# Three edits to a two-block kernel: full meta tile in the heads, final norm on three engines, gate and up as separate products

## The reference

```python
# attention: 8 heads, causal, keys are 16 meta tokens and 1024 others
p = softmax(where(kpos <= qpos, s, -inf));  o = p @ v
# experts: 64 of them, each token goes to 2
hh = silu(xb @ w_gate[e]) * (xb @ w_up[e])     # 1024 -> 256
y  = hh @ w_down[e]                            # 256 -> 1024
# end: the two expert rows of a token are added to h by their gates, then
return rmsnorm(h, final_norm_g)[:, N_META:]
```

## Time and profile before

| | |
|---|---|
| median of 3 runs | 2974.53 us (2974.14 to 2975.85) |
| the profiled execution, its own time | 2974.75 us |
| its span in the profile | 2973.0 us |
| TensorE busy | 2624.7 us, 88% |
| VectorE, ScalarE, GpSimd busy | 1038.2, 543.4 and 189.4 us |
| mean of the DMA engines | 190 GB/s |
| pairs of layer 0, first product to last | 1190.5 to 1699.7 us |
| pairs of layer 1, first product to last | 2408.7 to 2919.6 us |
| final norm | 2930.7 us to the end |

### The profile page before, as it was taken

One profiled execution on the slowest core, in us unless ns is written; L12 is line 12 of the kernel. 1 busy time (PEld: TensorE's weight loads), 2 busy tenths in 40 slices (PEclk: granted clock), 3 DMA queues, 4 the chain that ended last, 5 costly groups with the idle time before them and its releaser, 6 DMA issues. The chain is left out here.

```text
span 2973.0 us, 36737 instructions
## 1 busy us (share of the span) xinstructions
PE 2624.7 (88%) x14822; PEld 1477.7 (50%) x14822; DVE 1038.2 (35%) x2424; ACT 543.4 (18%) x1370; POOL 189.4 (6%) x262
## 2 busy tenths in 40 slices
PE   8999999998999997978877789999999978878882
PEld 3444579746888654333333255665665533333330
DVE  2424556556555344201111053444443431111114
ACT  0212455310000011201111031321221111111112
POOL 1000000000000000111111020000000011111100
PEclk9999999998999998988999889999999979999996
DMA  3101010131112154899999860000103479999995
GB/s 109 36 30 56 1 45 4 48 121 41 43 43 111 52 200 186 336 420 420 419 420 417 327 250 15 16 23 8 65 26 135 150 300 421 420 420 419 415 415 233
DMA packets 107724, 565.87 MB, mean 190 GB/s; under 512 B 21377, under 2 KB 21537, under 8 KB 56081
## 3 DMA queue, kind: packets, MB, share of 16 engines
q1 hardware_dynamic: 81216, 502.14, 42.4%
q0 software_dynamic: 21440, 43.51, 3.9%
q10 hardware_dynamic: 4896, 17.83, 1.5%
HBM read 529.06 MB, written 65.01 MB: 200 GB/s over the span
## 5 line engine op out<-in xcount | busy, mean ns | idle before, releaser
L2162 PE MATMUL ex__h_ps<-all__arena,ex__xT 128*64 128x512 f32 x1696 | 525.3, 674 | 170.8 <-DMA all__arena<-in_w_up 114.5
L2162 PEld LDWEIGHTS ex__h_ps<-all__arena,ex__xT 128*64 128x64 f32 x1696 | 169.9, 154 | 472.9 <-issue 468.3
L290 PE MATMUL fr__acc<-X__xT,fr__w 128*128 128x512 f32 x640 | 283.2, 603 | 7.5 <-DMA X__xT<-in_xT 7.5
L2190 DVE TENSOR_TENSOR ex__hs<-ex__sg,ex__h_ps 128x256 f32<-128x256 f32 x64 | 27.0, 421 | 680.6 <-ACT ex__sg L2187 680.3
L1290 PE MATMUL pb__acc<-b__w,all__arena 128*128 128x512 f32 x544 | 245.4, 606 | 9.3 <-POOL pb__eps L1250 9.3
L290 PEld LDWEIGHTS fr__acc<-X__xT,fr__w 128*128 128x128 f32 x640 | 122.6, 193 | 165.9 <-issue 156.6
L2162 PE MATMUL ex__h_ps<-mo__wx,ex__xT 128*64 128x512 f32 x352 | 178.0, 664 | 0.0
L1290 PEld LDWEIGHTS pb__acc<-b__w,all__arena 128*128 128x128 f32 x544 | 102.9, 194 | 129.2 <-issue 118.8
L2176 PE MATMUL ex__y_ps<-b__w,ex__hT 128*64 128x512 f32 x672 | 153.5, 598 | 1.1 <-ACT ex__hT L2193 1.1
L2187 ACT ACTIVATE ex__sg<-ex__h_ps 128x256 f32<-128x256 f32 x64 | 24.6, 384 | 656.2 <-PE ex__h_ps L2162 656.2
L1521 PE MATMUL cm__acc<-all__arena,cw__w 128*128 128x260 f32 x576 | 136.0, 386 | 2.3 <-PEq L84 2.3
(11 more groups left out here) (430 smaller groups left out, 3685.7 us busy)
## 6 DMA issues: line engine op xcount, KB each, us to landing
all__arena<-in_w_gate SPq DMA_DIRECT2D x106, 1024.0 KB, 21.6
all__arena<-in_w_up SPq DMA_DIRECT2D x106, 1024.0 KB, 25.5
b__w<-in_w_down SPq DMA_DIRECT2D x84, 1024.0 KB, 21.0
all__arena<-in_w_down SPq DMA_DIRECT2D x22, 1024.0 KB, 15.8
mo__wx<-in_w_down SPq DMA_DIRECT2D x22, 1024.0 KB, 25.4
mo__wx<-in_w_gate SPq DMA_DIRECT2D x22, 1024.0 KB, 23.9
mo__wx<-in_w_up SPq DMA_DIRECT2D x22, 1024.0 KB, 29.2
all__arena<-s_ys SPq DMA_DIRECT2D x16, 1024.0 KB, 7.7
```

What stands on the lines that cost most here:

```text
L290: last = mm(acc[:, b, c], wbuf[:, b, k], xT[:, k, 512 * c:512 * c + 512], start=(k == 0), stop=(k == KT - 1))
L2162: last = nc.tensor.matmul(h_ps[half, b].rearrange("p (a b) -> p a b", a=2), xT[:, b, k, half], slots[n][:, :, k], start=(k == 0), stop=(k ...
L2190: return nc.vector.tensor_tensor(hs[:, b], sg[:, b], h_ps[:, b, DE:], ALU.mult)
```

## The change

**Heads:** the meta keys are treated as a tile of 128 rows like the others: the transposed tile holds the 16 meta keys and the first 112 keys behind them, and the rows of `vv` that meet those 112 are zero (a memset once). Each group is then one copy. **Experts:** the product is split into `gate_products` and `up_products`, 16 calls of 256 columns each, with semaphores of their own; the down products of pair p-1 move between the two; SP loads gate of both experts when gate is done and up when up is done. ScalarE and VectorE follow this order. PSUM bank 0 holds gate, bank 1 up. **Final norm:** all eight tiles of `h` are loaded ahead, and four instead of three of the expert rows; ScalarE multiplies the tile with the inverted root, VectorE multiplies 384 columns with the gain (two tiles behind), and GpSimd the other 640; the stores move from GpSimd's queue to SP's.

The diff, cut to its core (the rest renames semaphores, passes them on, and makes the same split in code for overfull experts, which holds no product in the profile):

```diff
-            tiles = [(s, META + P * s, P) for s in range(i + 1)] + [(NB, 0, META)]
+            tiles = [(s, META + P * s) for s in range(i + 1)] + [(NB, 0)]
...
-                        at, r = (0, META) if tile == NB else (META + P * tile, P)
+                        at = 0 if tile == NB else META + P * tile
                         for k in range(CT):
-                            last = mm(t_ps[0:r, g % 2, 2 * VD * a:2 * VD * a + 2 * VD], ckv[:, k, at:at + r],
+                            last = mm(t_ps[:, g % 2, 2 * VD * a:2 * VD * a + 2 * VD], ckv[:, k, at:at + P],
                                       wkv[:, j % 2, k, 2:4].rearrange("p a b -> p (a b)"),
...
-                        for a, (s, at, r) in enumerate(group):
-                            last = nc.tensor.transpose(t_ps[0:r, q % 2, P * a:P * a + P], pr[:, h, u % 2, at:at + r], ident[:])
+                        for a, (s, at) in enumerate(group):
+                            last = nc.tensor.transpose(t_ps[:, q % 2, P * a:P * a + P], pr[:, h, u % 2, at:at + P], ident[:])
...
-                    for a, (s, at, r) in enumerate(tiles):
-                        last = mm(o_ps[:, h, 0:P], vv[0:r, s, h], pT[0:r, h, s], start=(a == 0), stop=(a == len(tiles) - 1))
+                    for a, (s, at) in enumerate(tiles):
+                        last = mm(o_ps[:, h, 0:P], vv[:, s, h], pT[:, h, a], start=(a == 0), stop=(a == len(tiles) - 1))
...
-                        full = [s for s, at, r in group if r == P]
-                        if full:
-                            last = nc.scalar.copy(pT[:, h, full[0]:full[-1] + 1].rearrange("p s q -> p (s q)"),
-                                                  t_ps[:, q % 2, 0:P * len(full)])
-                        if len(full) < len(group):
-                            at = P * len(full)
-                            last = nc.scalar.copy(pT[0:META, h, NB], t_ps[0:META, q % 2, at:at + P])
+                        last = nc.scalar.copy(pT[:, h, 4 * g:4 * g + len(group)].rearrange("p s q -> p (s q)"),
+                                              t_ps[:, q % 2, 0:P * len(group)])
...
+                v(V.memset(vv[:, NB].rearrange("p a b -> p (a b)"), 0.0))
...
+    def gate_in(sp, slot, e, loaded):
+        sp.dma_start(slot[:, 0], wg_d[bass.ds(e, 1)].rearrange("a (p k) f -> (a p) k f", k=KT)).then_inc(loaded, 16)
+
+    def up_in(sp, slot, e, loaded):
+        sp.dma_start(slot[:, 1], wu_d[bass.ds(e, 1)].rearrange("a (p k) f -> (a p) k f", k=KT)).then_inc(loaded, 16)
 
...
-        def gate_up_products(b, slots):
+        def gate_or_up_products(c, b, slots):
             for k in range(KT):
                 for n in range(2):
                     half = slice(CAP * n, CAP * n + CAP)
-                    last = nc.tensor.matmul(h_ps[half, b].rearrange("p (a b) -> p a b", a=2), xT[:, b, k, half],
-                                            slots[n][:, :, k], start=(k == 0), stop=(k == KT - 1))
+                    last = nc.tensor.matmul(h_ps[half, c, DE * b:DE * b + DE], xT[:, b, k, half], slots[n][:, c, k],
+                                            start=(k == 0), stop=(k == KT - 1))
             return last
+
...
-            return nc.scalar.activation(sg[:, b], h_ps[:, b, 0:DE], ACT.Silu)
+            return nc.scalar.activation(sg[:, b], h_ps[:, 0, DE * b:DE * b + DE], ACT.Silu)
...
-            return nc.vector.tensor_tensor(hs[:, b], sg[:, b], h_ps[:, b, DE:], ALU.mult)
+            return nc.vector.tensor_tensor(hs[:, b], sg[:, b], h_ps[:, 1, DE * b:DE * b + DE], ALU.mult)
...
+                    sp.wait_ge(m["g_done"], p - RING + 1)
+                    for n in range(2):
+                        gate_in(sp, gu_slots[r][n], p + n * PAIRS_M, g_loaded[r])
                     sp.wait_ge(m["h_done"], p - RING + 1)
                     for n in range(2):
-                        gate_up(sp, gu_slots[r][n], p + n * PAIRS_M, gu_loaded[r])
+                        up_in(sp, gu_slots[r][n], p + n * PAIRS_M, u_loaded[r])
                     sp.wait_ge(m["y_done"], p - RING + 1)
...
-                    pe.wait_ge(gu_loaded[p % RING], 64 * (p // RING + 1))
-                    gate_up_products(p % 2, gu_slots[p % RING]).then_inc(m["h_done"], 1)
+                    pe.wait_ge(g_loaded[p % RING], 32 * (p // RING + 1))
+                    gate_products(p % 2, gu_slots[p % RING]).then_inc(m["g_done"], 1)
+                    if p >= 1:
+                        last_product(p - 1)
+                    pe.wait_ge(u_loaded[p % RING], 32 * (p // RING + 1))
+                    up_products(p % 2, gu_slots[p % RING]).then_inc(m["h_done"], 1)
                     if p + 1 < PAIRS_M:
                         turn(p + 1)
-                    if p >= 1:
-                        last_product(p - 1)
                     pe.wait_ge(m["h_out"], p + 1)
                     turn_hidden(p % 2).then_inc(m["h_turned"], 1)
...
-                    act.wait_ge(m["h_done"], p + 1)
+                    act.wait_ge(m["g_done"], p + 1)
                     silu(p % 2).then_inc(m["silu_done"], 1)
+                    if p >= 1:
+                        y_half(p - 1)
                     if p + 1 < PAIRS_M:
                         rows_out(p + 1)
-                    if p >= 1:
-                        y_half(p - 1)
                     act.wait_ge(m["h_turned"], p + 1)
...
+                    if p >= 1:
+                        y_half(p - 1)
                     dve.wait_ge(m["silu_done"], p + 1)
+                    dve.wait_ge(m["h_done"], p + 1)
                     hidden(p % 2).then_inc(m["h_out"], 1)
                     if p + 1 < PAIRS_M:
                         rows_out(p + 1)
-                    if p >= 1:
-                        y_half(p - 1)
                     if p == 1:
                         gates(dve, v)
...
-    NBUF = 3
+    TT = SEQ // P
...
-        self.hb = part(0, self.NBUF, DM)
-        self.gb = part(3, DM)
+        self.hb = part(0, self.TT, DM)
+        self.gb = part(8, DM)
...
-        for t in range(self.NBUF):
+        for t in range(self.TT):
             sp.dma_start(self.hb[:, t], self.h_in[P * t:P * t + P]).then_inc(self.h_loaded[t], 16)
...
-        NBUF, NOUT = 3, 4
+        NBUF, NOUT = pre.NBUF, 4
+        CUT = 640
         yb, y_loaded = pre.yb, pre.y_loaded
         hb, gb, g_loaded, h_loaded = pre.hb, pre.gb, pre.g_loaded, pre.h_loaded
-        ho = part(15, NOUT, DM)
+        ho = part(17, NOUT, DM)
         sq = ph.sb("sq", [P, DM], mybir.dt.bfloat16)
         ss, rt, rs = (ph.sb(n, [P, 2]) for n in ("ss", "rt", "rs"))
         eps = ph.sb("eps", [P, 1])
-        eps_done, made, squared, rooted, scaled, v_own = (
-            ph.sem(n) for n in ("eps_done", "made", "squared", "rooted", "scaled", "v_own"))
+        eps_done, made, squared, rooted, inverted, normed, scaled, part_scaled, v_own = (
+            ph.sem(n) for n in ("eps_done", "made", "squared", "rooted", "inverted", "normed", "scaled", "part_scaled", "v_own"))
         stored = [ph.sem(f"o{n}_stored") for n in range(NOUT)]
         with nc.Block() as block:
 
             @block.sync
             def _(sp):
                 for t in range(TT):
-                    b = t % NBUF
-                    if t >= NBUF:
-
-                        sp.wait_ge(made, t - NBUF + 1)
-                        sp.dma_start(hb[:, b], h_in[P * t:P * t + P]).then_inc(h_loaded[b], 16)
-                        pre.rows_in(sp, t)
+                    if t + NBUF < TT:
+
+                        sp.wait_ge(made, t + 1)
+                        pre.rows_in(sp, t + NBUF)
+                    sp.wait_ge(scaled, t + 1)
+                    sp.wait_ge(part_scaled, t + 1)
+                    sp.dma_start(D["out"][P * t:P * t + P], ho[:, t % NOUT]).then_inc(stored[t % NOUT], 16)
+                for b in range(NOUT):
+                    sp.wait_ge(stored[b], 16 * ((TT + NOUT - 1 - b) // NOUT))
 
             @block.gpsimd
             def _(pool):
+                pool.wait_ge(g_loaded, 16)
                 for t in range(TT):
-                    pool.wait_ge(scaled, t + 1)
-                    pool.dma_start(D["out"][P * t:P * t + P], ho[:, t % NOUT]).then_inc(stored[t % NOUT], 16)
-                for b in range(NOUT):
-                    pool.wait_ge(stored[b], 16 * ((TT + NOUT - 1 - b) // NOUT))
+                    pool.wait_ge(normed, t + 1)
+                    nc.gpsimd.tensor_tensor(ho[:, t % NOUT, 0:CUT], ho[:, t % NOUT, 0:CUT], gb[:, 0:CUT],
+                                            ALU.mult).then_inc(part_scaled, 1)
 
             @block.scalar
             def _(act):
                 act.wait_ge(eps_done, 1)
                 nc.scalar.activation(rt[:, 1:2], eps[:], ACT.Sqrt)
-                for t in range(TT):
-                    b = t % 2
-                    act.wait_ge(made, t + 1)
-                    if t >= 2:
-                        act.wait_ge(scaled, t - 1)
```

(47 more changed lines are left out.)

39 lines of the change are left out of this document (24 added, 15 removed).

## The result

The changed kernel takes 2946.9 us, the median of 4 runs (2945.6 to 2948.1), against 2974.3 us (2973.6 to 2975.9) before: ratio 0.9907, 95% interval 0.9891 to 0.9923. The forecast was 2962.1 us in a range of 2954 to 2973. The direction was right, the time lies 7 us under the range, and the gain is 27.5 us where 12.2 were forecast.

What follows compares the result with a forecast made beforehand. Weight transfers were taken to pace the experts' stretches, TensorE nearly always busy in the heads. 2973.0 - 8.0 - 7.1 (experts) - 1.5 (heads) + 4.2 (norm) = 2960.6 us profiled, 2962.1 in runs; range 2954 to 2973.

Steps and rivals of the forecast that it cites:

- Mixing products have equal columns: Heads: mixing products keep their column count, so the change was given no effect on their time.
- 1.5 us net: Heads: fewer copies save 2.8 us, wider transposes cost about 1.3; net gain 1.5 us, between -3 and +8.
- The waits of TensorE for ScalarE: Heads: TensorE's waits for ScalarE were to fall by 2 to 3 us.
- E: Rival, chance 0.10: norm's ScalarE multiply or tail is shorter, or heads give their 8 us: 2952 to 2957 us.
- GpSimd's multiply ... fits under 4.57: Norm: GpSimd's 640 columns take 2.2 us at the end, 3 to 4 inside, within a tile's cycle of 4.57.
- VectorE is stretched too: Norm: VectorE's multiply-adds lengthen beside GpSimd, 0.2 us by 5, +1.0 us in all.
- rival B: Norm, chance 0.12: GpSimd blocks VectorE for its whole instruction, second multiply-adds wait, +12 to +24 us: 2974 to 2986 us.
- Rows 12: Profile rows cited for the norm: a VectorE multiply-add of 1.28 us took 1.54 beside GpSimd, argued against full blocking.
- Experts, start: Experts: first down product and its reload come 4.6 us earlier; 4.0 us gained a layer, 8.0 in all.
- Rival D: Experts, chance 0.11: early start is lost as transfers run out again some pairs later; only the ends gain: 2970 us.
- Experts, end: Experts: last down product 8.7 us after the last up lands, against 11.5 and 13.0; gain 7.1 us.
- Rival C: Experts, chance 0.05: 256-column products don't hide weight loads or issue; over 0.33 us for two, TensorE bounds; +190 us at 0.43.

Runs made afterwards that it cites:

- run 2: Kernel before, with only the mixing products reading all 128 rows of the meta tile, transposes and copies unchanged: 2952.0 us, ratio 0.9918.
- run 4: Kernel before, with the second head's mixing starting at its 16-row tile, so both heads' 16-row products stand side by side: 2961.5 us, ratio 0.9952.
- run 1: Kernel before with the whole heads' part of the change alone: 2951.0 us, ratio 0.9921.
- run 3: Kernel before with the heads' part, but mixing products still reading only 16 rows of the meta tile: 2973.4 us, ratio 0.9997.
- run 10: As run 3, but mixing reads 64 rows of the meta tile: 2973.3 us, ratio 0.9996.
- run 8: Changed kernel, with VectorE's part of the norm's gain copied once into PSUM, GpSimd's multiply unchanged: 2943.4 us, ratio 0.9887.
- Run 11: Kernel before with the experts' part alone, but down products left behind the up products and next transposes: 2968.5 us, ratio 0.9977.
- run 5: Kernel before with the final norm's part of the change alone: 2984.9 us, ratio 1.0030.
- run 6: Kernel before with the experts' part of the change alone: 2959.4 us, ratio 0.9946.
- run 7: Changed kernel, with VectorE multiplying all 1024 columns by the gain and GpSimd doing nothing in the norm: 2938.7 us, ratio 0.9872.
- run 9: Changed kernel, with VectorE alone making the norm's sums and scaling, ScalarE only square and root, GpSimd nothing: 2931.0 us, ratio 0.9857.

## Why the prediction was wrong, and where it was right

**Heads: the step that failed.** "Mixing products have equal columns" put mixing at nothing. The columns are equal, the row counts were not: TensorE went 128, 16, 128 rows twice in a block of queries, and each change cost it 0.18 to 0.19 us (runs 2 and 4, and the single products shown above). 32 blocks with four changes are 128 changes, 23.6 us, the term that is missing. It was to be seen before: the two forms of L1887 differed by 38 ns at equal columns, and two blocks of different length left 0.7 us that the instruction count did not explain. The profile page's own group of that line mixes them ("+1 forms", 290 ns), so they have to be asked for by form. What I did price there fits: 1.5 us net was forecast for copies and transposes, runs 1 and 2 differ by 1.5, and run 3 gives 0.9; but unchanged heads scatter by 0.9, so this is no close test, and the way to it was wrong. The waits of TensorE for ScalarE did not fall by 2 to 3 us as forecast: in the heads those of L1877 and L1887 are 16.5 us in all after the change and were 17.0. The time lies under all the rivals too: the lowest, E, began at 2952 us and gave the heads 8 us.

Not all changes are gone: counted over the order of products in the trace, the heads' stretch had 208 changes between 128 rows and fewer, and has 80 now, at 64-row products. At one of them, among the score products, the start-to-start time again grows from 0.12 to 0.22 us. No run took these away.

The Trainium skill has the rule, and I did not weigh it: the page TensorEngine Tiling (Array Packing) (section "Key Properties") says that changing the tiling mode, and not merely the tile, drains TensorE. Runs 2, 4 and 10 agree with that and give it a price, 0.18 to 0.19 us at 128 columns; that the price is a drain no run here shows by itself.

**Norm: direction right, size wrong.** From the first multiply-add to the end +9.4 us, +4.2 forecast. The step was "GpSimd's multiply ... fits under 4.57" and "VectorE is stretched too": +1.0 for all tiles. In fact, where GpSimd's multiply starts first, here by 0.02 us, VectorE stands still until it is done. A tile is then 2.51 us (made to normalised, on ScalarE), 0.08 of handoff, 1.53 of GpSimd, 0.34 for the rest of VectorE's multiply, 1.27 for the second multiply-add and 0.04: 5.77. That is 1.2 us over my 4.57, six times. From the last made (the end of a tile's second multiply-add) to the end of the span I had 3.2 more; it is 2.3 (11.8 against 9.5). This is rival B, which I gave 0.12, in mechanism. In the first tile it stands where B put it, at the second multiply-add (2.55 us); in the next five, at VectorE's multiply ahead of that. Its price is smaller, since GpSimd's 640 columns take 1.53 us, below my lower bound of 2.2. That bound came from a GpSimd instruction with one tensor input, and so did the row by which I argued against B: the stretch of 1.28 to 1.54 was measured beside an instruction of another kind.

The page SBUF — State Buffer of the Trainium skill (section "SBUF: two separate sides") states the lock that I argued down: a VectorE instruction with two SBUF inputs against a GpSimd one that reads SBUF, the second fully blocked. Here the trace agrees: 1.92 against 0.56 us, and run 8 moves the wait to the next instruction of that kind by moving one input to PSUM. Rows 12 do not agree: there GpSimd's one-input instruction began first, at 1721.09, and ran to 1722.60, yet VectorE's multiply-add, begun at 1721.58, was done at 1723.12, where a full wait would have ended it no earlier than 1722.60 + 1.28 = 1723.88. Whether GpSimd's second input makes that difference no run tested. The estimate from the GPSIMD Engine Reference of the Trainium skill, 1.4 us for 640 columns, was nearer to the measured 1.53 than my rows.

**Experts, start: right.** The down reload comes 4.4 us earlier (4.6). Rival D falls: the stream empties once (a DMA share of 0.39 from 1211 to 1213) and is full again soon (0.97 from 1214 to 1216, 1.00 from 1216 to 1218). Run 11 confirms that this gain hangs on the early down products.

**Experts, end: right in kind, mis-sized at two points.** To the last down product the layers gain 8.1 and 9.5 us where 6.8 and 8.3 were forecast. I counted 8.7 us from the landing of the last ups. The last up transfer landed 31.4 us after its issue at 1652.1 at the latest, so at 1683.5, and the last down product starts 6.7 us later:

```profile
L2075 SPq DMA_DIRECT2D mo__wx<-in_w_up x1: 6961/6961/6961, 1652.1 to 1652.1; - x1
DMA to landing us min/median/max: 18.2/30.0/31.4
```

The down products of the pair before do not wait for the ups, they follow the gates: the chain from the landing of the gates is 3.5, 3.4, 3.5 and 1.7 us, 12.1 in all, and the ups fall into it. I had put these products behind the ups. In layer 1 it is 8.9 us, near my 8.7, but for another reason: there TensorE, after 4.6 us without work, did the gates mostly at half its clock (granted 0.52 from 2864.6 to 2868), 5.1 us instead of 3.5, and the ups, landed at 2869.4, waited for it until 2873.1. What is left of the gain, and belongs to the start and the stream, is then 3.3 us in layer 0 and 5.4 in layer 1, where I had 4.0 for each; that the sum fits better than its parts is luck. Against it stands what I did not count: in layer 0 the last pair's scatter needs longer to land. From its issue to SP's next load that waits for it, timeline before:

```profile
1701.61 0.98 POOL L2318 DMA_INDIRECT s_ys<-ex__ysb,mo__queue  x1 [4.05 <-DVE ex__ysb L2199]
...
1705.06 1.28 SPq L2527 DMA_DIRECT2D all__arena<-s_ys  x3
```

and after:

```profile
1695.49 0.97 POOL L2326 DMA_INDIRECT s_ys<-ex__ysb,mo__queue  x1 [7.69 <-DVE ex__ysb L2203]
...
1701.35 0.80 SPq L2540 DMA_DIRECT2D all__arena<-s_ys  x2
```

3.45 us have become 5.86: 2.4 us given back, 0.6 in layer 1 by the same measure. The products now end sooner than the next phase's loads, which are queued ahead of the scatter. That it waits for these is argued from their order in layer 0. In layer 1 runs show it, since there the norm's part sets how many loads are queued, and the experts' part how early the scatter comes:

| layer 1 | last queued load landed, from the scatter's issue | the scatter's issue to SP's next load |
|---|---|---|
| before | 7.8 us earlier | 3.2 us |
| run 5: more loads alone | 1.4 us earlier | 3.2 us |
| run 6: earlier scatter alone | 3.8 us earlier | 3.2 us |
| changed kernel: both | 2.9 us later | 3.8 us |
| run 7: both | 4.9 us later | 5.7 us |
| run 8: both | 5.1 us later | 5.7 us |
| run 9: both | not in the trace | 5.7 us |

I had looked only at whether the loads would land before the norm's first instruction. They do; the step that I put at nothing is the scatter behind them in the queue.

**Rival C** falls by the 3.67 us of 32 products: two side by side take about 0.21 us, not 0.33.

**Sum.** On the profiled execution 12.4 us were forecast and 27.7 came, 15.3 more: 24.3 from the heads and 2.5 from the experts' products, less 5.2 in the norm, 2.8 between the experts' last product and the next phase, and 3.5 in stages that nothing touched.

## What to carry to other kernels

Instructions of one accumulation that differ in row count are priced by the changes between them, not by their own columns: read such a line by form, and take the length of two blocks of different size apart into a price per instruction and a remainder. Padding with zero rows was the cheap way here; putting the odd ones side by side saved half.

Before work is given to GpSimd, ask whether both engines would run instructions with two SBUF inputs at that moment: here the helper's time then lay on VectorE's, and dropping it and closing VectorE's own gaps was worth 15 us in a stage of 51. A row used as a bound must be of the same kind of instruction, inputs included, or it bounds nothing.

When one part of a change ends a stage earlier and another queues more loads ahead of its last transfer, look at the two together: in layer 1 neither alone lengthened the way from the last scatter's issue to the next load, and both together did by 0.6 to 2.5 us.

## What the runs showed of the hardware that I had not expected

A change between 128-row and 16-row neighbouring products of 128 columns costs TensorE 0.18 to 0.19 us in either direction, and the same with 64 rows. A VectorE multiply of 384 columns with two SBUF inputs takes 0.56 us alone, 0.55 beside GpSimd with one input in PSUM, and 1.92 with both in SBUF when a two-input GpSimd instruction starts just before it. GpSimd's multiply of 640 columns with two inputs takes 1.53 us, 2.4 ns a column, where its one-input instruction of 320 had shown 1.08 us; VectorE takes 1.22 us for 1024.
